# A decoder layer with a state-space branch: u and y change layout through DRAM instead of on TensorE

## The reference

```python
xn = rmsnorm(x, norm_g)
u_a, z_a, q, k, v, z_b, g_a, g_b = split(xn @ w_in)          # 2048 -> 10240
y_a, h_last = s5_scan(u_a, h0, A, log_dt, B, C, D)           # 64 groups of 16 channels, state of 64 complex numbers
y_a = gelu(y_a); y_a = y_a * sigmoid(y_a @ glu_w + glu_b) * silu(z_a)
o = stick_breaking_attention(q, k, v) * silu(z_b)            # 8 heads of 128
merged = sigmoid(g_a) * (y_a @ w_branch_a) + sigmoid(g_b) * (o @ w_branch_b)
out = rmsnorm(x + merged @ w_out, norm_f)

def s5_scan(u, ...):                                         # for each group g
    a_bar = exp(lam * dt); b_bar = (a_bar - 1) / lam * B
    h[t] = a_bar * h[t-1] + b_bar @ u[t]                     # complex, over the tokens t
    y[t] = real(C @ h[t]) + D * u[t]
```

## Time and profile before

| | us |
|---|---|
| median of 3 runs (3100.43 to 3104.88) | 3103.77 |
| the profiled execution's own time | 3098.39 |
| its span | 3096.3 |
| PE busy, share of the span | 3031.6, 98% |
| DVE, ACT, POOL busy | 1330.4, 1010.5, 468.6 |
| DMA queue of SP, share of 16 engines | 33.0% |

### The profile page before, as it was taken

How to read it: one execution, slowest core, us unless ns; L and a number is a source line. 1 busy time by engine, 2 the same in 40 slices (tenths; PEclk the granted TensorE clock), 3 DMA queues, 4 the chain that set the end, 5 groups by cost and what they waited for, 6 DMA issues and landing times.

```text
span 3096.3 us, 49157 instructions
## 1 busy us (share of the span) xinstructions
PE 3031.6 (98%) x19548; PEld 2940.4 (95%) x19548; DVE 1330.4 (43%) x2539; ACT 1010.5 (33%) x1261; POOL 468.6 (15%) x1126
## 2 busy tenths in 40 slices
PE   6999999999999999999999999999999999999997
PEld 5999999999999999999999999999999889999997
DVE  6624443452444345244435524443565123422266
ACT  6135214413621541352153135225421111212142
POOL 6400330140033014003202300410013000000000
PEclk8999999999999999999999999999999999999999
DMA  6232223223122222212222221322449655242283
GB/s 178 56 98 69 68 62 96 71 65 96 62 76 67 88 66 73 88 62 76 80 83 58 75 86 62 83 87 69 143 145 299 197 164 164 86 139 68 78 242 110
DMA packets 400898, 312.41 MB, mean 101 GB/s; under 512 B 58338, under 2 KB 365106, under 8 KB 398642
## 3 DMA queue, kind: packets, MB, share of 16 engines
q1 hardware_dynamic: 400690, 309.44, 33.0%
HBM read 227.30 MB, written 65.27 MB: 94 GB/s over the span
## 4 chain that ended last, share of the span: by engine, by line
PE 91%; DVE 4%; ACT 2%; issue 1%; POOL 0%; DMA 0%; SPq 0%; DVEq 0%; POOLq 0%; ACTq 0%
PE acc L1701 80%; PE side L1666 3%; PE side L1869 2%; PE side L1924 1%; PE side L1864 1%; DVE work L1456 1%; PE side L1800 0%; PE side L1799 0%; ACT w_high L834 0%; PE side L1811 0%; PE side L1982 0%; DVE work L1463 0%; DVE work L1457 0%; DVE x_low L1316 0%; DMA work<-in_x_prompt 0%
## 5 line engine op out<-in xcount | busy, mean ns | idle before, releaser
L1701 PE MATMUL acc<-x_high,w_high 128*128 128x344 f32 (+2 forms) x5440 | 1223.4, 328 | 17.8 <-ACT w_high L834 4.0
L1701 PE MATMUL acc<-x_low,w_high 128*128 128x344 f32 (+2 forms) x5440 | 1180.2, 320 | 0.0
L1701 PE MATMUL acc<-x_high,w_low 128*128 128x344 f32 (+2 forms) x5440 | 1176.5, 319 | 0.0
L1701 PEld LDWEIGHTS acc<-x_high,w_high 128*128 128x128 f32 x5440 | 905.5, 188 | 41.9 <-issue 21.8
L1701 PEld LDWEIGHTS acc<-x_low,w_high 128*128 128x128 f32 x5440 | 920.9, 189 | 0.0
L1701 PEld LDWEIGHTS acc<-x_high,w_low 128*128 128x128 f32 x5440 | 912.3, 188 | 0.0
L834 ACT CAST w_high<-w_raw 128x1024 fp32r<-128x1024 f32 x232 | 242.2, 1044 | 952.5 <-PE acc L1701 881.0
L1301 DVE TENSOR_TENSOR w_low<-w_raw,w_high 128x1024 fp32r<-128x1024 f32 x233 | 289.8, 1244 | 547.8 <-ACT w_high L834 545.1
L1172 POOL COPY work<-s_tables 128x28 f32 x16 | 3.3, 206 | 1547.4 <-DMA work<-t_state_seeds 1355.6
L1449 DVE TENSOR_TENSOR work<-work,side 128x128 f32<-128x128 f32 x64 | 18.4, 287 | 317.5 <-PE side L1869 317.5
L1666 PE MATMUL side<-work 128*128 128x128 f32 (+5 forms) x704 | 136.1, 311 | 0.0
(11 more groups left out here) (308 smaller groups left out, 2495.2 us busy)
## 6 DMA issues: line engine op xcount, KB each, us to landing
w_raw<-in_w_in SPq DMA_DIRECT2D x160, 512.0 KB, 3.8
w_raw<-in_w_out SPq DMA_DIRECT2D x48, 512.0 KB, 3.9
work<-t_sig_ga SPq DMA_DIRECT2D x24, 516.0 KB, 4.5
out<-work SPq DMA_DIRECT2D x18, 512.0 KB
t_qk<-stage SPq DMA_DIRECT2D x16, 516.0 KB, 5.0
work<-t_qk SPq DMA_DIRECT2D x16, 516.0 KB, 4.5
t_sig_gb<-stage SPq DMA_DIRECT2D x16, 516.0 KB, 4.1
t_sig_ga<-stage SPq DMA_DIRECT2D x16, 516.0 KB, 4.1
```

The source lines that it names most:

```text
L1701: ins = mm(acc[s][:, a, 0:n], w[b][:, kk, :], x[:, kx, c0:c0 + n], start=start, stop=stop)
```

## The change

u no longer goes through PE. ACT writes it with the offset outermost (all blocks of offset 0, then of offset 1; the new tokens are block 128). SP stores it to DRAM (`t_u`) and reads it back in 16 transfers: eight of 16 channels x 8 groups x 128 blocks for Ug, eight of one element per channel and group for the new tokens (Us). PE's state products of half 0 wait for all 16 (L1798 in the changed kernel). XJ, UG and US are gone on PE and ACT.

In the output products the operands change places, so that (offset, channel) is on the partitions of the result and the block in the columns. ACT copies it in one piece per half; SP stores it by eight transfers per half (`y_rows`) and, after both halves, reads all back (`y_back`). YT on PE keeps only the one product for the new tokens, now at step 38 (YN); DVE adds D u at step 40 after `y_back`, ACT takes gelu at step 41.

```diff
-    Ug = c.take(8 * NCH).rearrange("p (g j) -> p g j", g=8)
+    yT = c.take(8 * NCH)
+    Ug = yT.rearrange("p (g j) -> p g j", g=8)
+    u_off, y_off = uT.rearrange("p (t j) -> p t j", t=CH), yT.rearrange("p (t j) -> p t j", t=CH)
...
+            def u_groups():
+                sp.wait_ge(u_ready, i + 1)
+                sp.dma_start(t_u, uT).then_inc(u_sent, 16)
+                sp.wait_ge(u_sent, (i + 1) * 16)
+                rows = t_u.rearrange("(g c) (t j) -> t c g j", c=GC, t=CH)
+                for tau in range(CH):
+                    sp.dma_start(Ug[tau * GC:(tau + 1) * GC], rows[CH - 1 - tau][:, :, 0:NCH]).then_inc(ug_in, 16)
+                for t in range(CH):
+                    sp.dma_start(Us[:, :, t:t + 1], rows[t][:, :, NCH:NCH + 1], allow_slow_non_contiguous=True).then_inc(ug_in, 16)
+            def y_rows(hf):
+                sp.wait_ge(yj_ready, i * 2 + hf + 1)
+                rows = t_yj.rearrange("(g c) (t j) -> t c g j", c=GC, t=CH)
+                for t in range(CH):
+                    sp.dma_start(rows[t][:, hf * HG:(hf + 1) * HG],
+                                 xy[t * GC:(t + 1) * GC, hf * 512:(hf + 1) * 512].rearrange("p (g j) -> p g j", g=HG)).then_inc(yj_sent, 16)
+            def y_back():
+                sp.wait_ge(yj_sent, (i + 1) * 256)
+                sp.dma_start(yT, t_yj).then_inc(yj_in, 16)
                 if cn == 3:
+                    u_groups()
                     toeplitz(0)
                 if cn == 6:
+                    y_rows(0)
                     s5_states(0)
                     s5_seeds(1)
                 if cn == 10:
+                    y_rows(1)
                     s5_states(1)
+                    y_back()
...
-                nc.scalar.copy(tok3(uT), acc_v(0)).then_inc(u_ready, 1)
+                nc.scalar.copy(uT.rearrange("p (t b j) -> p b j t", t=CH, b=NB), acc_v(0).rearrange("p b (j t) -> p b j t", t=CH)).then_inc(u_ready, 1)
-                        for g in range(HG):
-                            dst = xy[:, 0:SEQ].rearrange("p (t f) -> p t f", t=CH)[:, :, hf * 64 + g * GC:hf * 64 + (g + 1) * GC]
-                            last_op = nc.scalar.copy(dst, side[:, 0, g * P:(g + 1) * P].rearrange("p (t c) -> p t c", t=CH))
-                        last_op.then_inc(yj_ready, 1)
+                        nc.scalar.copy(xy[:, hf * 512:(hf + 1) * 512], side[:, 0, :]).then_inc(yj_ready, 1)
...
-                    for a in range(2):
-                        yv, uv = [z[:, 0:SEQ].rearrange("p (j t) -> p t j", t=CH)[:, 4 * a:4 * a + 4, :] for z in (xy, uT)]
-                        last_op = V.scalar_tensor_tensor(yv, uv, dcol[:, bass.ds(i, 1)], side[:, a, :].rearrange("p (t j) -> p t j", t=4), ALU.mult, ALU.add)
+                    dve.wait_ge(yj_in, i * 16 + 16)
+                    V.scalar_tensor_tensor(xy[:, 0:SEQ].rearrange("p (j t) -> p t j", t=CH), u_off[:, :, 0:NCH], dcol[:, bass.ds(i, 1)],
+                                           y_off, ALU.mult, ALU.add).then_inc(yt_ready, 1)
...
                     if p == PQ[hf]:
+                        pe.wait_ge(kt_ready, 2 * i + hf + 1)
                         if hf == 0:
-                            pe.wait_ge(us_ready, i + 1)
-                        else:
-                            pe.wait_ge(kt_ready, 2 * i + 2)
+                            pe.wait_ge(ug_in, i * 256 + 256)
-                            mm(out, Ug[:, HG * hf + g, :], Toep[:, g, :], start=True, stop=False)
-                            mm(out, V1[:, g, 0:NCH], N1[:, g, GC:9 * GC], start=False, stop=True)
+                            mm(out, Toep[:, g, :], Ug[:, HG * hf + g, :], start=True, stop=False)
+                            mm(out, N1[:, g, GC:9 * GC], V1[:, g, 0:NCH], start=False, stop=True)
-                if p == XJ:
-                if p == UG:
-                if p == US:
```

More of the change, by code:

```diff
@@ L147, in build @@
     t_qs = dram("t_q_new", [NEW, WIDTH])
+    t_u, t_yj = dram("t_u", [P, TOK]), dram("t_y_by_offset", [P, SEQ])
     t_n, t_h = dram("t_output_seeds", [2, P, WIDTH]), dram("t_state_seeds", [2, P, GROUPS * NEW])
@@ L265, in build @@
     den_ready, consts_in = sem("den_ready"), sem("consts_in")
-    act_chain, pool_consts, us_mm, us_ready, br_a, br_b, h_rstd, new_done = [sem(s) for s in
-        ("act_chain", "pool_consts", "s5_us_mm", "s5_us_ready", "branch_a_used", "branch_b_used", "h_rstd", "new_rows_done")]
+    act_chain, pool_consts, br_a, br_b, h_rstd, new_done = [sem(s) for s in
+        ("act_chain", "pool_consts", "branch_a_used", "branch_b_used", "h_rstd", "new_rows_done")]
     g_in_rows, xs_in = sem("norm_g_rows_in"), sem("x_new_in")
@@ L279, in build @@
         ("s5_b_mm", "s5_bt_ready", "s5_k_mm", "s5_kt_ready", "s5_kt_pad", "s5_toep_in")]
-    xj_mm, xj_ready, ug_mm, ug_ready, pq_mm, v_ready, y_mm, yj_ready, fin_ready, p_copied, t_ready, swap_in = [sem(s) for s in
-        ("s5_xj_mm", "s5_xj_ready", "s5_ug_mm", "s5_ug_ready", "s5_pq_mm", "s5_v_ready", "s5_y_mm",
+    u_sent, ug_in, yj_sent, yj_in, pq_mm, v_ready, y_mm, yj_ready, fin_ready, p_copied, t_ready, swap_in = [sem(s) for s in
+        ("s5_u_sent", "s5_ug_in", "s5_yj_sent", "s5_yj_in", "s5_pq_mm", "s5_v_ready", "s5_y_mm",
          "s5_yj_ready", "s5_fin_ready", "s5_p_copied", "s5_scanned", "s5_swapped_in")]
@@ L407, in phase_a @@
                 sp.lower_val((i + 1) * 128 * 4)
+                sp.lower_val((i + 1) * 256)
             def ahead(cn):
@@ L734, in build @@
     TURN, BT, KM, PQ, SCAN, ROT, YM, YS = (4, 20), (8, 24), (11, 27), (13, 30), (15, 32), (17, 34), (18, 36), (19, 37)
-    XJ, UG, US, YT = 9, 10, 12, 38
+    YN, YT = 38, 40
     VT, NTR, KTR, ZB_AT = 45, 46, 57, 44
@@ L875, in phase_a @@
                         nc.scalar.copy(SO, side[0:NEW, 0, :].rearrange("p (g s) -> p g s", g=HG)).then_inc(ys_ready, 1)
-                if p == XJ:
[L877 to L882, removed]
-                if p == UG:
-                    act.wait_ge(ug_mm, i + 1)
-                    nc.scalar.copy(Ug, side_flat.rearrange("p (g j) -> p g j", g=8)).then_inc(ug_ready, 1)
-                if p == US:
-                    act.wait_ge(us_mm, i + 1)
-                    nc.scalar.copy(Us, side[0:GC, 0, 0:64].rearrange("p (g b) -> p g b", g=8)).then_inc(us_ready, 1)
-                if p == YT + 2:
+                if p == YT + 1:
                     act.wait_ge(yt_ready, 2 * i + 2)
@@ L1431, in phase_a @@
                 if p == YT:
-                    dve.wait_ge(yt_mm, 2 * i + 1)
-                    for a in range(2):
-                        yv, uv = [z[:, 0:SEQ].rearrange("p (j t) -> p t j", t=CH)[:, 4 * a:4 * a + 4, :] for z in (xy, uT)]
-                        last_op = V.scalar_tensor_tensor(yv, uv, dcol[:, bass.ds(i, 1)], side[:, a, :].rearrange("p (t j) -> p t j", t=4), ALU.mult, ALU.add)
[L1436 to L1439, removed]
+                    dve.wait_ge(yt_mm, i + 1)
+                    V.scalar_tensor_tensor(xy[:, SEQ:TOK], u_off[:, :, NCH], dcol[:, bass.ds(i, 1)], side[:, 0, 0:NEW], ALU.mult, ALU.add).then_inc(yt_ready, 1)
+                    dve.wait_ge(yj_in, i * 16 + 16)
+                    V.scalar_tensor_tensor(xy[:, 0:SEQ].rearrange("p (j t) -> p t j", t=CH), u_off[:, :, 0:NCH], dcol[:, bass.ds(i, 1)],
+                                           y_off, ALU.mult, ALU.add).then_inc(yt_ready, 1)
                 if p == KTR:
@@ L1777, in phase_a @@
                         pe.wait_ge(n_ready, 2 * i + hf + 1)
-                        if hf == 0:
-                            pe.wait_ge(ug_ready, i + 1)
-                        else:
-                            pe.wait_ge(bt_ready, 2 * i + 2)
+                        pe.wait_ge(bt_ready, 2 * i + hf + 1)
                         for g in range(HG):
@@ L1812, in phase_a @@
                         last_op.then_inc(ys_mm, 1)
[L1813 to L1830, removed]
-                    pe.wait_ge(ys_ready, 2 * i + 2)
[L1832 to L1836, removed]
+                if p == YN:
+                    pe.wait_ge(ys_ready, 2 * i + 2)
                     one(side[:, 0, 0:NEW], ysT, ident[0:NEW, 0:NEW]).then_inc(yt_mm, 1)
```

## The result

| | before | after |
|---|---|---|
| median of six runs each, us | 3102.72 (3099.19 to 3104.88) | 3164.36 (3160.07 to 3168.65) |
| span of the profiled execution, us | 3096.3 | 3163.0 |
| mean granted clock of PE, share of full speed | 0.995 | 0.983 |

The changed kernel takes 1.0199 times as long, 95% interval 1.0186 to 1.0212: 61.6 us more. The forecast was 3182, 78 us more, with a range of 3142 to 3222. The direction and the mechanism came as forecast, the size 18 us smaller.

A forecast was written before the change was run, and what follows sets the result against it. The kernel was taken to be bound by PE's chain of waits. Profiled 3098.4 us + 78.6 (u path) - 7.0 (step 38) + 2.4 (seeds) + 4.0 (attention loads) = 3176.4; 5.4 more for the median: 3182, range 3142 to 3222.

The forecast's parts named there:

- Where the u path starts: In SP's queue, the store of u stands behind chunk 3's weight load, which waits for DVE's low half: 363.95 us, tile 1.
- The u path's length: Store, 16 loads and landing before step 13: store 5.0 us, issues 0.65 apart, landing 2.3; Ug complete at 381.0, tile 1.
- PE from there to the output products: PE after Ug is complete: 15.07 us as before plus 1.7 for the halved clock, reaching them at 397.8 in tile 1.
- The sum of the two: Low half to output products: 34.4 us in tile 1, 9.0 later than before; 78.6 us over eight tiles.
- Both chains equally late: At the output products of tile 1, DVE's rotation ends at 397.0, PE arrives at 397.8; a smaller step 13 wait helps little.
- Rival C: One-element loads of u issued at the price of D's column, 0.49 us more each, 31 in all: 3213; chance 0.15.
- A: Rival: the transfers are hidden and only the removal is left, 25.0 us less: 3079; chance 0.08.
- B: Rival: u's loads issued 0.34 us apart, 37 us less in all: 3145; chance 0.12, including anything between it and A.
- Seeds behind the stores of y: Group 0's eight y stores delay half 1's seeds; POOL starts 2.9 us later against 2.6 margin: 2.4 us in all.
- Transposes of step 38: PE's transposes at step 38 are gone: 0.88 x 8 = 7.0 us gained.
- Attention loads: After y's way through DRAM, the loads come 1.4 us later and PE waits: 0.5 us per tile, 4 in all.
- The exchanged operands: Output products keep 128 loaded and 128 moving columns, still 0.22 us per pair: nothing counted.

The follow-up runs named there:

- u_early: The changed kernel with SP issuing the store of u and its 16 loads before it waits for the low half of chunk 3: 3089.31 us, 0.9959.
- y_alone: Only the y part of the change on the kernel before, u still turned by PE and ACT: 3105.58 us, 1.0007.
- u_early_seeds_first: As u_early, and SP loads the seeds of half 1 before it stores the y rows of half 0: 3079.68 us, 0.9925.
- us_own_wait: The changed kernel with a separate semaphore for the eight one-element loads, so PE's state products wait for eight loads, not sixteen: 3182.50 us, 1.0262.
- both kernels with a busy PE: 64 identity transposes on PE ahead of its wait for Ug, on the changed kernel and on it with seeds before y's stores: 3176.78 and 3161.58 us.
- toeplitz_first: As us_own_wait, and SP issues the eight Toeplitz transfers before the eight one-element loads: 3189.03 us, 1.0282.

## Why the prediction came out as it did

**Where the u path starts: right.** SP came to the store of u only after DVE's low half and the weight load, 0.6 us behind the half's end (375.30) in tile 1. u_early shows that this place is the cause.

**The u path's length: forecast 3 us too long.** Forecast 17.05 us from SP's being free to a complete Ug, measured 14.0 in tile 1 (375.89 to 389.88), 13.7 to 14.0 in tiles 0 to 6 and 15.6 in the last. The term that failed is the issue of the sixteen loads, 0.65 us apart by the Toeplitz transfers. They came 0.47 apart: 15 x 0.18 = 2.7 us. The Toeplitz transfers have the same 16 partitions but go from SBUF to SBUF; the loads read DRAM. The nearest row was another: the two loads of seeds, also from DRAM, in 1.02 us, 0.51 apart. That the source decides is not shown: the bias (0.34) and D's column (1.14) come from DRAM as well. The landing was 1.8 instead of 2.3 us. The store took 5.1, forecast 5.0.

**PE from there to the output products: 1.2 us too short.** Forecast 16.8 (15.07 and 1.7 for the clock), measured 17.94 in tile 1 (389.88 to 407.82) and 17.2 to 17.9 in the others. The low clock costs 2.2 to 2.9 us per tile and not 1.7.

**The sum of the two.** From the low half to the output products 34.4 forecast, 32.5 measured. Against before that is +9.0 forecast and +7.3 measured in tile 1; over eight tiles 78.6 and 65.1. The last tile came at +9.6 (10.3), this near only because its store took 6.7 us, where the others took 5.0 to 5.2. Tile 0 came at +12.7 (12.6), but by two errors that cancel. From its low half to the output products it took 31.6 us (100.03 to 131.60), 2.8 less than forecast; the low half itself came 2.8 later relative to BT0 than before (16.3 against 13.5 us). DVE had waited 9.9 us for POOL's preparation ahead of its turning factors, against 7.2, and PE waited for DVE (timeline of PE; the earlier trace rows has DVE's half before):

```profile
100.17 1.20 PE L1713 MATMUL acc<-x_high,w_high 128*128 128x344 f32 x3 [6.34 <-DVE w_low L1316]
```

y_alone and u_early have the same later POOL in tile 0 (10.2 and 9.9 us), u_early_seeds_first has not (7.2). It is not the u path. In ten of the twelve profiled executions this wait is 9.9 to 10.4 us, whatever the edit, so it may be a difference between executions and not between kernels; one profile of each cannot tell.

**Both chains equally late: right.** The prediction had DVE at 397.0 and PE at 397.8, and said that a smaller wait at step 13 alone would help little. us_own_wait shows it (28 us less waiting, none of it gained), and both kernels with a busy PE do. So the clock is real but not a term of its own: it stretches PE's side of a tie that DVE holds as well. The Trainium skill (TensorE: Matmul & The Clock Gate, Why this matters for your kernels) advises against idle gaps of PE, since the clock falls back behind them. The trace agrees on the fall (0.50 in the windows above), but filling the gap gained 2.8 and 2.0 us in the stretch here and nothing in the whole kernel.

**Rival C: wrong.** The one-element loads are issued at the price of the 64 KB ones, 3.74 us against 3.65 for eight (in toeplitz_first, behind the Toeplitz transfers, 3.90 to 5.09). The Trainium skill (DMA: Bandwidth & Descriptors, Rules for kernel authors) says that a non-contiguous last dimension makes one descriptor per element; the 128 elements of such a load landed in 1.7 us and 64 KB in 2.2. This does not test the rule: the 64 KB load has 128 contiguous pieces too (16 channels x 8 groups), of 512 bytes each. It shows only that pieces of 4 bytes were no dearer than pieces of 512.

**Rivals A and B.** A does not hold where the path stands, but u_early_seeds_first reaches its 3079 (3079.68) once the path starts ahead of the weight load: A's condition was the whole matter, and its price was right to 2 us (23.0 below the kernel before, forecast 25.0; between the two profiled executions the stretches give 18.5). The 50 ns of the Trainium skill (DMA: Bandwidth & Descriptors, Anatomy of one DMA), on which A leans, stand there for DMAs that GpSimd issues; here SP issues them, 0.47 us apart. B's 0.34 us was too low; the truth, 0.47, lies between it and the forecast, and so does the time (3145, 3164, 3182).

**Seeds behind the stores of y: too small.** Forecast 2.4 us, measured +7.5 in BT1 to YM1. In tiles 1, 2, 5 and 6 it is 0.4, near the 0.3 worked out for tile 1. In tiles 0, 3 and 4 it is 1.3 and in the last 1.7, and there PE waits for POOL, as in tile 4 (timeline of PE):

```profile
1265.91 1.05 PE L1678 MATMUL side<-work 128*16 128x128 f32 x8 [1.28 <-POOL work L1206]
```

The margin of 2.6 us was read rightly: in all eight tiles of the kernel before POOL has N ready 27.95 us after the start of the output products of half 0, and PE comes at 30.54. The term that failed is how long POOL takes from the seeds to N, which the forecast left as it was. POOL starts on the seeds 2.4 us later than before in tile 1 (forecast 2.9). From there to N it took 10.8 us, and takes now 11.1 to 11.2 in tiles 1, 2, 5 and 6 and 12.2 to 12.3 in the others. There one of POOL's operations is about 1 us slower than its like and falls inside N; in tile 1 it falls just behind N (timeline of POOL, tile 1 and then tile 4; POOL's spans are rough, but PE's wait agrees):

```profile
437.74 0.41 POOL L1205 TENSOR_TENSOR work<-work 128x64 f32<-128x64 f32 x1
...
438.69 1.19 POOL L1238 TENSOR_TENSOR work<-work 128x32 f32<-128x32 f32 x1
...
1264.17 1.30 POOL L1205 TENSOR_TENSOR work<-work 128x64 f32<-128x64 f32 x1
```

In y_alone and u_early the slow operation falls inside N in seven tiles, and just these are 1.3 to 1.6 us longer in BT1 to YM1. It stands some 30 us after the start of the output products; in the kernel before, POOL is through by then. The later seeds used up the margin and moved N to where it stands. What makes the operation slow no trace shows.

**Transposes of step 38: right.** YM1 to VT is 7.0 us shorter.

**Attention loads: forecast 4.0, measured none.** PE never waits for them. Relative to YM1 the store of y is issued 1.9 us later than before in tile 1, but it lands in a median of 2.7 us instead of 4.0. SP's weight load was issued 1.1 us ahead of it before and is 3.4 us ahead now. The loads are so issued only 0.3 us later, within the margin. The gelu table was loaded while ACT waited, as forecast (timeline of ACT):

```profile
481.18 1.28 ACT L906 ACT_TABLE_LOAD   x1
484.76 1.07 ACT L906 ACTIVATE work<-work 128x1032 f32<-128x1032 f32 x1 [2.30 <-DVE work L1450]
```

**The exchanged operands: right**, 0.22 us a pair as before.

In short, the forecast of 3182 was 17.6 us too high. The u path makes 13.5 of them and the attention loads 4.0, while the seeds were 5.1 too low: 12.4 together, against 11.4 between the sum (3176.4) and the profiled execution's own time (3165.0). The other 6.2 are the step from an execution to the median: I added 5.4 and 0.2 by rounding, and the median lies 0.7 below the profiled execution.

## What to carry to other kernels

Before pricing transfers that take over work from PE, find what stands ahead of their first issue in the issuing queue: here a loss of 62 us and a gain of 23 differ by two calls moved a few lines. Where two engines arrive at the same moment, relieving one buys nothing, and moving a load in the queue only chooses which of the two is late, while taking it out helps both. A margin that a forecast delay just uses up is no margin: one operation of POOL that was 1 us slower than its like was covered before and is paid now.

## What the runs showed of the hardware

- SP's issue of eight 16-partition DMAs took 3.65 us for rows of 512 bytes from DRAM to SBUF, 3.74 for single elements, 3.66 to 3.88 back to DRAM (stores of y, tile 1), and 5.22 to 6.03 from SBUF to SBUF (Toeplitz, tile 1). It is no fixed price: behind the Toeplitz transfers (toeplitz_first) eight single-element loads took 3.90 to 5.09.
- The same 516 KB store lands in a median of 5.1 us when it is issued 0.4 us behind a weight load (t_u after) and of 2.7 when that load is 12 us back (t_u in u_early, below, in its list of DMA issues):

```profile
t_u<-work SPq DMA_DIRECT2D x8, 516.0 KB, 2.7
```

- ACT's copy of u with a stride takes twice as long as a plain one of that size, 2.08 against 1.02 us (timeline of ACT, after). Other work covered it:

```profile
364.36 2.08 ACT L843 COPY work<-acc 128x1032 f32<-128x1032 f32 x1
...
400.21 1.02 ACT L857 COPY stage<-acc 128x1032 f32<-128x1032 f32 x1
```

- Two idle times of 3.3 and 3.6 us in tile 1 (us_own_wait) were each followed by the lower clock (0.50), and one of 6.7 us in tile 1 after the change by one such stretch: there, splitting the wait cost more clock than it had as one.
- POOL has single operations about 1 us slower than their like: before the change one in each tile, 9.3 us after YM0 (L1183, 1.38 us where its like take 0.40), and after it a second, near 30 us (L1205 in tile 4, 1.30 against 0.41 in tile 1). Where the second fell inside N, BT1 to YM1 lost 1.3 to 1.7 us, and where it fell just behind it, 0.4.
